# A two-block transformer kernel: in the MLP's first two weight pairs VectorE makes more low parts and reads results sooner, the down weights' sums move up, and half a gate tile moves between attention groups

## The reference

```python
attn = dsa_attention(...)          # top-k selected keys, 8 heads
y_b = attn @ w_b
m = g[:, :, 0] * y_a + g[:, :, 1] * y_b + g[:, :, 2] * y_c      # g = sigmoid(g_raw + b_gate)
h = h + m @ w_o
hn = rms_norm(h, norm2_g)
gate, up = jnp.split(hn @ w_gate_up, 2, axis=-1)                # D_FF = 2816
return h + (jax.nn.silu(gate) * up) @ w_down
```

## Time and profile before

| | us |
|---|---|
| median of 3 runs | 2262.42 |
| lowest, highest | 2260.57, 2264.54 |
| the profiled execution, whole | 2263.33 |
| its span in the profile | 2261.6 |
| PE busy in the span | 2177.1 |
| DVE, ACT, POOL busy | 1423.0, 915.9, 1026.8 |

### The profile page before, as it was taken

One profiled execution on the slowest core, in us unless ns is written; L12 is line 12 of the kernel. 1 busy time (PEld: TensorE's weight loads), 2 busy tenths in 40 slices (PEclk: granted clock), 3 DMA queues, 4 the chain that ended last, 5 costly groups with the idle time before them and its releaser, 6 DMA issues.

```text
span 2261.6 us, 29882 instructions
## 1 busy us (share of the span) xinstructions
PE 2177.1 (96%) x10752; PEld 1798.1 (80%) x10752; DVE 1423.0 (63%) x2788; ACT 915.9 (40%) x1627; POOL 1026.8 (45%) x580
## 2 busy tenths in 40 slices
PE   6999999999999989999989999999999999999998
PEld 6886688998887778778867888888888878888886
DVE  4248799999932466655597566665567736206844
ACT  5234522223225674433442233333445554226743
POOL 1265433455544233225656555555588623121063
PEclk8999999999999999999999999999999999999999
DMA  5112111111224213036524445455876331111031
GB/s 189 45 48 75 57 47 48 51 53 37 70 84 131 75 48 98 29 98 185 188 66 139 164 144 177 144 177 172 299 237 205 112 112 48 47 47 38 30 130 75
DMA packets 243829, 238.46 MB, mean 105 GB/s; under 512 B 10337, under 2 KB 186110, under 8 KB 243694
## 3 DMA queue, kind: packets, MB, share of 16 engines
q1 hardware_dynamic: 239536, 223.49, 30.7%
q10 hardware_dynamic: 4158, 13.16, 1.4%
HBM read 174.54 MB, written 61.15 MB: 104 GB/s over the span
## 4 chain that ended last, share of the span: by engine, by line
PE 76%; DVE 7%; issue 3%; ACT 2%; POOL 1%; ACTq 0%; DVEq 0%
PE ps L981 23%; PE ps L1268 17%; PE ps L1296 9%; PE ps L1342 9%; PE ps L1158 6%; PE ps L1563 4%; PE ps L1541 2%; PE ps L1190 1%; PE ps L1133 1%; DVE logit L2400 1%; PE ps L1176 1%; PE ps L1526 1%; PE ps L1510 1%; DVE pt_lo L2419 0%; PE ps L1500 0%
## 5 line engine op out<-in xcount | busy, mean ns | idle before, releaser
L3028 POOL TENSOR_TENSOR w_lo<-w_raw,w_hi 128x1024 fp32r<-128x1024 f32 (+1 forms) x129 | 296.3, 2298 | 744.1 <-ACT w_hi L1592 744.1
L981 PE MATMUL ps<-x_hi,w_hi 128*128 128x512 f32 (+2 forms) x960 | 360.8, 376 | 4.0 <-DVE c_rs L2317 3.3
L981 PE MATMUL ps<-x_lo,w_hi 128*128 128x512 f32 (+2 forms) x960 | 359.1, 374 | 0.0
L981 PE MATMUL ps<-x_hi,w_lo 128*128 128x512 f32 (+2 forms) x960 | 357.1, 372 | 0.0
L981 PEld LDWEIGHTS ps<-x_hi,w_hi 128*128 128x128 f32 x960 | 180.9, 188 | 39.7 <-issue 9.3
L981 PEld LDWEIGHTS ps<-x_hi,w_lo 128*128 128x128 f32 x960 | 181.2, 189 | 28.7
L981 PEld LDWEIGHTS ps<-x_lo,w_hi 128*128 128x128 f32 x960 | 180.7, 188 | 28.6 <-issue 0.2
L2375 DVE MATCH_REPLACE8 score<-best,score 128x400 f32<-128x400 f32 (+3 forms) x224 | 185.0, 827 | 0.0
L2371 DVE MAX8 best<-score 128x8 f32<-128x400 f32 (+3 forms) x224 | 181.1, 841 | 1.4
L1592 ACT CAST w_hi<-w_raw 128x1024 fp32r<-128x1024 f32 (+1 forms) x129 | 127.7, 991 | 103.8 <-PE ps L981 73.0
L1268 PE MATMUL ps<-x_hi,wr_hi 128*128 128x512 f32 x352 | 139.9, 398 | 2.8 <-DVE x_lo L2524 2.0
(11 more groups left out here) (473 smaller groups left out, 5444.9 us busy)
## 6 DMA issues: line engine op xcount, KB each, us to landing
w_raw<-in_w_in SPq DMA_DIRECT2D x74, 512.0 KB, 3.8
wdr<-as_scratch SPq DMA_DIRECT2D x77, 256.0 KB, 3.9
rawg<-in_w_gate_up SPq DMA_DIRECT2D x22, 512.0 KB, 4.0
rawu<-in_w_gate_up SPq DMA_DIRECT2D x22, 512.0 KB, 5.4
wdr<-in_w_down SPq DMA_DIRECT2D x22, 512.0 KB, 6.6
as_scratch<-ac SPq DMA_DIRECT2D x44, 256.0 KB, 3.9
wt_scratch<-wdr SPq DMA_DIRECT2D x33, 256.0 KB, 4.7
as_scratch<-a SPq DMA_DIRECT2D x33, 256.0 KB, 3.9
```

The costliest lines, as they stand in the source:

```text
L981: mm = pe.matmul(ps[:, b, 0:n], w[:, s, P * k:P * k + P], r[:, k, t0:t0 + n], start=k == 0 and i == 0, stop=k == kd - 1 and i == 2 and ext ...
L3028: pool.tensor_tensor(w_lo[:, p % 2, 0:n], w_raw[:, p % 2, 0:n], w_hi[:, p % 2, 0:n], ALU.subtract).then_inc(wlo_done, 1)
```

## The change

1. `x_low` on DVE no longer skips even tiles: tiles 16 to 27 (the inputs of P5, P6 and P3) are all made by DVE, and POOL's six calls for them are gone. Tiles 0 to 15 are shared as before.
2. DVE's block_low(13) and combined_weights(2), which stood ahead of the reads of pairs 0 and 1, stand behind the third read of pair 0 and behind all eight reads; block_low(15) goes behind combined_weights(2). combined_weights(3) goes from the start of pair 2 to behind that pair's first read.
3. ACT's cast of a P1 or P2 block no longer waits for that pair's sums.
4. POOL's down_combined(0) moves from behind block 20's low part to between those of blocks 14 and 16. Its tile `wt1` lies elsewhere, so it no longer waits for the products of pair 1.
5. The second half of the last gate tile (`AROUND[8]`) is computed ahead of group 9's turns instead of behind group 8's, and its finish on ACT and on POOL moves to the start of group 9.

The tile `wt1`, and PE's order in attention:

```diff
-        wt1 = place("wt1", [P, BANK], F32, ST + 24 * S)
+        wt1 = place("wt1", [P, BANK], F32, W_RAW + 48 * S)
...
-                if g in AROUND and g != 9:
+                if g == 9:
+                    dense(AROUND[8], (1,))
+                elif g in AROUND:
                     dense(AROUND[g], (0,))
...
-                if g in AROUND:
+                if g in AROUND and g != 8:
                     dense(AROUND[g], (1,) if g != 9 else (0, 1))
```

On ACT, the group loop (POOL's is changed alike, with `behind`), and the wait in `block_high`:

```diff
+                if g == 9:
+                    evict(AROUND[8])
                 high_part(g, 0)
                 high_part(g, 1)
...
-                if g in AROUND:
+                if g in AROUND and g != 8:
                     evict(AROUND[g])
...
-                    if n >= 2 or prod not in ("P1", "P2"):
+                    if prod not in ("P1", "P2"):
                         act.wait_ge(tw_done, TW_DONE_0 + 4 * n + 4)
```

On DVE, `x_low`, the first pairs and `gate_up_pair`:

```diff
             def x_low(y):
-                if y % 2 == 0:
-                    return
                 dve.wait_ge(xh_done, y + 1)
+                if y == 16:
+                    dve.wait_ge(*low_x(14))
...
             block_low(9)
-            x_low(17)
-            x_low(19)
+            for k in range(16, 20):
+                x_low(k)
...
-            x_low(25)
-            x_low(27)
-            block_low(13)
-            combined_weights(2)
+            for k in range(24, 28):
+                x_low(k)
             for n in range(2):
...
+                if n == 0:
+                    block_low(13)
                 dve.tensor_tensor(g1[n][:, :], g1[n][:, :], ps[:, bank_of(n, "P4"), :], ALU.add).then_inc(po_done, 1)
-                if n == 0:
-                    block_low(15)
+            combined_weights(2)
+            block_low(15)
...
-                if n + 1 < FC:
+                if n + 1 < FC and n > 2:
                     combined_weights(n + 1)
...
                         dve.tensor_tensor(a[0][:, :], r1[0][:, :], result("P6"), ALU.add).then_inc(po_done, 1)
+                        if n == 2:
+                            combined_weights(n + 1)
```

On POOL:

```diff
             block_low(10)
-            x_low(16)
-            x_low(18)
-            x_low(20)
-            x_low(22)
             block_low(12)
-            x_low(24)
-            x_low(26)
             block_low(14)
+            down_combined(0)
             block_low(16)
...
-                    if (n, i) in ((2, 0), (2, 6)):
-                        pool.wait_ge(am_done, AM_DONE_0 + 4)
-                        down_combined(i // 6)
+                    if (n, i) == (2, 6):
+                        down_combined(1)
```

More of the change, by code:

```diff
@@ L2609, in _ @@
             block_low(11)
-            x_low(21)
-            x_low(23)
+            for k in range(20, 24):
+                x_low(k)
             for k in range(4):
@@ L3162, in _ @@
                     behind(BEFORE[g])
-                if g in AROUND:
+                if g == 9:
+                    behind(AROUND[8])
+                if g in AROUND and g != 8:
                     behind(AROUND[g])
@@ L3223, in _, with down_combined @@
                         x_low(6)
+            def down_combined(j):
+                pool.wait_ge(wd_load, WD_LOAD_0 + 32 * j + 32)
+                pool.tensor_tensor(wt1[:, :], wdr[:, 1, :], wdr[:, 0, :], ALU.subtract).then_inc(wdt_done, 1)
+                pool.wait_ge(wdt_done, WDT_DONE_0 + 4 * j + 1)
+                pool.tensor_tensor(wdr[:, 1, :], wdr[:, 3, :], wdr[:, 1, :], ALU.subtract).then_inc(wdt_done, 1)
+                pool.wait_ge(wdt_done, WDT_DONE_0 + 4 * j + 2)
+                pool.tensor_tensor(wdr[:, 0, :], wdr[:, 1, :], wdr[:, 0, :], ALU.add).then_inc(wdt_done, 1)
+                pool.wait_ge(wdt_done, WDT_DONE_0 + 4 * j + 3)
+                pool.tensor_tensor(wdr[:, 2, :], wdr[:, 2, :], wdr[:, 0, :], ALU.subtract).then_inc(wdt_done, 1)
             block_low(6)
@@ L3247, in _ @@
                 pool.tensor_tensor(a_st[0][n][0][:, :], a_st[0][n][0][:, :], g0[n][:, :], ALU.mult).then_inc(am_done, 1)
-            def down_combined(j):
-                pool.wait_ge(wd_load, WD_LOAD_0 + 32 * j + 32)
-                pool.tensor_tensor(wt1[:, :], wdr[:, 1, :], wdr[:, 0, :], ALU.subtract).then_inc(wdt_done, 1)
-                pool.wait_ge(wdt_done, WDT_DONE_0 + 4 * j + 1)
-                pool.tensor_tensor(wdr[:, 1, :], wdr[:, 3, :], wdr[:, 1, :], ALU.subtract).then_inc(wdt_done, 1)
-                pool.wait_ge(wdt_done, WDT_DONE_0 + 4 * j + 2)
-                pool.tensor_tensor(wdr[:, 0, :], wdr[:, 1, :], wdr[:, 0, :], ALU.add).then_inc(wdt_done, 1)
-                pool.wait_ge(wdt_done, WDT_DONE_0 + 4 * j + 3)
-                pool.tensor_tensor(wdr[:, 2, :], wdr[:, 2, :], wdr[:, 0, :], ALU.subtract).then_inc(wdt_done, 1)
             for n in range(2, FC):
```

2 lines of the change are left out of this document (1 added, 1 removed).

## The result

The changed kernel takes 2267.99 us (median of 20 runs, 2265.55 to 2272.92), the kernel before 2264.47 on the same chips (20 runs, 2259.36 to 2267.74). The ratio is 1.0019, 95% interval 1.0012 to 1.0026: slower by 3 to 6 us. The forecast was 4.6 us faster.

The account below looks back on a forecast made before the run. PE, busy for 96% of the span, was taken as the bound, with time lost in its holes or at half clock. -4.2 + 2.1 - 2.8 + 0.3 = -4.6 gave a 2257.8 us median, range 2252.5 to 2262.5.

Parts of the forecast that it names:

- Group 9's division ... -2.8: Attention: group 9's division ends at 844.35 us, not 847.16, 2.8 us sooner; PE then waits 2.9 before the turns.
- I charge +0.3, between 0 and 2.8: Attention: mh loads, queued behind a weight load, land at 860 to 861; DVE waits about 1 us, charged +0.3.
- rival C: Attention gives nothing: mh loads land late and DVE hands the 2.8 us back; -2.1 overall, 2260.3 us; 22%.
- The table load ... nothing on the path: Attention, group 9: the exponential's table load delays it by 1.1 us, which later casts absorb; nothing on the path, or 0.3.
- Up to the third read ... -6.0: MLP start: DVE's third read starts at 1178.0 us instead of 1184.03, 6.0 us sooner.
- POOL still meets it twice (blocks 10 and 12), 2.3 us: MLP start, before the third read: POOL's work on SBUF slows DVE at two blocks, costing DVE 2.3 us.
- rival D: Slower: down weights land late, from about 1182 on, so down sums meet DVE's sums; about 2264 us; 8%.
- From there to L2705 ... 28.8: MLP, DVE from third read to the read for pair 2's last block: 28.8 us instead of 27.0, net -4.2.
- PE meanwhile: MLP: PE starts block 12 at 1178.8 and block 13 at 1182.9, then runs seven products without a wait to 1202.4.
- A longer wait ... 5.2: MLP, pair 2's last block: PE waits 5.2 us for L2705 instead of 2.22, and half clock follows.
- carried through unchanged: MLP's later pairs, 1212 to 1740 us: PE stays full, so gains or losses of the first pairs pass through.
- edits at nothing: MLP edits said to give nothing by themselves: ACT's cast of block 14 without its wait, wt1's place, the down weights' issue.

Follow-up runs that it names:

- e3: The kernel before with item 5 only, and SP's queries, gates and mh loads issued ahead of the weight load that waits for POOL: 2261.36 us against 2264.51.
- e6: The kernel before with item 1 only (tiles 16 to 27 made low by DVE): 2268.93 us against 2264.19.
- e9: e6, with DVE waiting for POOL's low part of block 12 ahead of the last round of differences: 2259.06 us against 2263.75.
- e7: e5 with item 4 undone (pair 0's down sums again behind block 20, old tile wt1): 2262.03 us against 2264.19.
- e2: The changed kernel with item 5 undone, attention as before: 2266.43 us against 2264.51.
- e4: e2 with DVE's read P6 ahead of the next pair's sums in odd pairs from 3 on: 2262.51 us.
- e5: e2 with item 3 undone from pair 3 on, so ACT's casts wait for the sums again: 2261.14 us against 2264.19.

## Why the prediction was wrong

By its steps:

- *"Group 9's division ... -2.8"*: right. The wait was 2.79 where 2.9 was said, and e3 keeps 2.9 us of it.
- *"I charge +0.3, between 0 and 2.8"* for the `mh` loads: the step that failed. The queue was named, and its start was right: SP issued the weight load at 850.65, which is 849.06 on the clock of before, and DVE wanted the loads at 859.13 on it. Wrong was the time that the queue takes. The forecast had 3.6 MB at 324 GB/s, 11.1 us; it took 14.1 (850.65 to 864.77). In the first microsecond nothing moved, and behind it 4.15 MB went at 316 GB/s, since SP issued a further weight load of half a megabyte at 860.35, while the `mh` loads were under way. DVE waited 4.05 and not "about 1", the lead that the forecast gave PE did not cover it, and PE's wait of 3.48 us was followed by a lower clock of its own (0.66 over five microseconds). Attention ended 3 to 4 us later than where it was left alone, and not 2.5 sooner: 6 us of the error. The rival C had this mechanism, and too low a price.
- *"The table load ... nothing on the path"*: right; the load took 1.28 us at 859.98 and the exponential began 1.30 later. In the changed kernel DVE's wait would have covered it, but e3 has no such wait and keeps the 2.9.
- *"Up to the third read ... -6.0"*: measured 7.3 sooner, for DVE met POOL but once.
- *"POOL still meets it twice (blocks 10 and 12), 2.3 us"*: wrong in kind. DVE paid nothing at block 12, and POOL paid 6.2 us. Pair 2's weights and the down weights were issued 4.1 us later than before, where "two or three us sooner" was said; the down weights were used at 1190.91, or 1185.3 on the clock of before, where the forecast had them landed by 1178.5. This is rival D's condition ("from about 1182 on"), and its place is partly D's: the first down sum met the last sum of combined_weights(2), the others the low parts of blocks 15, 17 and 19. D had 8%, since the forecast took the length of a meeting as DVE's to pay and not as POOL's. e6 and e9 show the cause.
- *"From there to L2705 ... 28.8"*: it took 32.6. Missing were the waits of 1.05 for weights and 3.14 for block 18; the second I had not in the list, although combined_weights(3) waits for that block in the code and I had moved 4 instructions of POOL ahead of it. So -1.7 instead of -4.2. e7 shows that undoing that move by itself gives only 0.7.
- *"PE meanwhile"*: the waits before blocks 12 and 13 were 1.60 and 0.27, not 2.5 and 1.3, since the reads came sooner still. *"Seven products ... follow without a wait"* is wrong: they held 3.5 us of waits, for blocks 14, 15 and 16.
- *"A longer wait ... 5.2"*: measured 5.32, by luck. PE arrived 2.5 us later than forecast and L2705's counterpart came 2.5 later, and the two errors cancel. *"+2.1"* of half clock: right, 2.0.
- *"carried through unchanged"* and ACT's cast among the *edits at nothing*: wrong, by 2.8 us (4.4 in e2). Its cover was named for block 14 only, but the edit holds for all pairs: 1.1 us ahead of one read in every other pair, which PE feels where the down weights land late as well. e4 and e5 show it.

The changed kernel's sum by these: -1.7 + 2.0 + 2.8, and 3 for attention, make +6; the runs say +3 to +6.

## What to carry to other kernels

Where a weaker engine's one instruction releases a queue of loads, look at how long the stronger engine's row of back-to-back SBUF work beside it is, and leave a gap: 1.2 us idle on DVE took 6.3 off its wait for weights in e9 (3.6 of the MLP's time against e6). When a wait is deleted, list every place at which the loop makes it, and ask what it kept apart there. When work that releases a DMA moves, follow SP's queue to the last load behind it, count what else is issued while these loads are under way, and set the moment at which the last one lands against the moment at which it is wanted.
